# Token-major output projections with resident split weights in a two-layer hybrid decoder kernel

## The chip, the cores and the metric

The kernel is one program for one core of a Trainium2 chip. A core has a matrix engine (TensorE, PE in the rows, with PEld for its weight loads), VectorE (DVE), ScalarE (ACT), GpSimd (POOL) and SyncE (SP), which here mostly issues DMAs. The engines run their own instruction streams and meet at semaphores. The metric is device time in microseconds (us) of one execution. TensorE's clock has two levels, 1.2 and 2.4 GHz, and the profile gives the granted share of the upper one.

## The reference

A prompt of 1024 tokens and 8 samples of 8 tokens pass two layers, each `x + Mixer(RMSNorm(x))`, and a last RMSNorm. The kernel puts them side by side as T = 1088 tokens. What the change touches is the end of each mixer and what follows it:

```python
def rmsnorm(x, g):                       # x * rsqrt(mean(x^2) + 1e-6) * g
def retention_layer(...):                # layer 0
    ...
    o, s_new = chunked_linear_recurrence(q, k, v, log_a, s0)      # 4 heads, 512 values each
    o = _rms(o).reshape(b, L, 2048) * head_norm                   # one norm per head
    return (o * silu(gate)) @ w_out, s_new                        # w_out (2048, 1024)
def ssd_layer_full(...):                 # layer 1
    ...
    y, s_new = chunked_linear_recurrence(cm, bm, v, log_a, s0)    # 8 groups, 256 values each
    g = (y + xs * d_skip) * silu(z)
    g = _rms(g.reshape(b, L, 8, 256)).reshape(b, L, 2048) * gate_norm
    return g @ w_out, s_new, new_conv
def trunk(...):
    h = h + retention_layer(rmsnorm(h, ret_norm), ...)
    h = h + ssd_layer_full(rmsnorm(h, ssm_norm), ...)
    return rmsnorm(h, final_norm), ...
```

## The kernel before

Everything is float32. Large products are split: each operand is a high part rounded to the type fp32r and a low part, the remainder, and three fp32r matmuls (high x high, high x low, low x high) are summed. The program (`program`) runs its phases one after the other. Each phase is a block with one instruction stream per engine, and its end is a barrier for all of them.

Activations lie channel-major: the 128 partitions are channels, tokens run along the row, and in DRAM a tensor is (channels, T).

- `phase_input` turns x with TensorE, and its result is also written to `xT_dram` as the residual.
- `phase_project` (lines 230 to 610) is used four times (tags p1 to p4). It takes one block of 128 output channels after the other. For a block it loads the weights for all K input blocks, splits them (ScalarE copies to `whi`, VectorE subtracts to `wlo`, lines 376 and 524, two slots), and TensorE multiplies for every input block, pass and each of four stretches of 272 tokens (line 471). The weights are the stationary operand, the tokens stream. For p2 and p4 (K = 16, 8 output blocks) VectorE then adds the residual block (line 590) and SP stores it to `h1_dram` or `h2_dram`, channel-major.
- `phase_retention` goes through 4 heads x 8 chunks of 128 tokens, plus one chunk of 64 sample tokens per head, so 36 units, each with `y` in PSUM. VectorE gates it (line 1064, `r_gn`), ScalarE squares it, GpSimd and a ones-matmul sum the squares, ScalarE makes the root (Ln and Exp, lines 922 and 925), VectorE multiplies by it (line 1070, `r_gf`), ScalarE copies to `ghi` (line 929), and GpSimd subtracts to `glo` (line 995). `ghi` and `glo`, the split input of the next projection, stay in SBUF for all T tokens. GpSimd had multiplied the gates by the head norm before (line 990).
- `phase_norm_steps` loads `h1`, norms it (`norm_parts`: squares on ScalarE, pair sums on VectorE, ones-matmuls, root, then per block norm, high copy, and subtraction, alternately on VectorE and GpSimd at line 170), and computes the SSD step sizes from 32 columns of the input projection (line 1271).
- `phase_ssd` goes through 8 groups of 4 heads, 8 chunks plus a sample chunk each: 72 units. Per chunk VectorE makes the masks (lines 1748, 1750), adds the state (1826), the sample state (1808), forms the outputs (1770 to 1780) and the decayed scores (1761), and norms the chunk before (line 1799, `s_gf`). GpSimd makes values (1672), decays the state (1698), gates (1685, `s_gn`), scales the sample state (1715) and subtracts to `g2lo` (1689). On SP a chunk is four loads for the chunk four ahead and the sample state for the chunk two ahead (line 1416, slots `s_in`); each waits first, the former for `gated`, the latter for the use of the slot (`held`, which waits and adds one to a counter).
- `phase_output` loads `h2` by tiles of 128 tokens, turns them with TensorE, makes squares and root on ScalarE, norms on VectorE (line 1939) and stores y.
- `clear_semaphores` clears all semaphores that are in use, one instruction each on SP, in a block of its own; it is called once, after p2.

## Time and profile before

| | us |
|---|---|
| median of 3 runs (lowest, highest) | 2537.31 (2534.93, 2539.39) |
| the profiled execution: its time | 2532.14 |
| its span, first to last instruction | 2530.4 |

| stage | from, us | length, us |
|---|---|---|
| input, norm, p1 | 0 | 636 |
| retention | 636 | 334 |
| p2 | 970 | 201 |
| norm and SSD steps | 1171 | 80 |
| p3 | 1251 | 595 |
| SSD | 1846 | 447 |
| p4 | 2293 | 201 |
| output | 2494 | 36 |

Over the span TensorE is busy 88% (2238.6 us), VectorE 41%, ScalarE 31%, GpSimd 20%, and 291.87 MB are moved at a mean of 115 GB/s. A share over the whole span mixes stages with different limits, so the stages have to be read one by one. In the rows by stretches the columns are: stretch, length, busy us with instructions in brackets for PE, PEld, DVE, ACT and POOL, then the granted clock, the DMA engines' busy share, and GB/s. In timelines a row may merge several instructions of a kind (xN), and brackets at the end name the idle time before and what ended it. Matmul records are pipelined and overlap; their pace is read from the distance of their starts.

### The profile page before, as it was taken

Reading aid. Unit: us, or ns where it says so; the run is one execution under the profiler, and the core shown is the slowest. Engines: PE = TensorE matmul, PEld = TensorE weight load, DVE = VectorE, ACT = ScalarE, POOL = GpSimd, SP = SyncE. Lnnn points to the kernel's source line nnn. Section 1 sums busy time; section 2 is a strip of 40 time slices with the busy share of each in tenths; the row PEclk is TensorE's granted clock in tenths of the full one; section 3 lists DMA queues with packets and bytes.
Section 4 is the critical chain, followed back from the end, with each engine's and each line's share of the span. In section 5 each row is a group of like instructions: output and inputs, shape, how many; then the busy total and the mean of one; then the engine's idle time right before and its main releaser. Section 6 shows DMA issues by size and latency. Waiting matters only on the chain. (4 is left out here: it accounts for less than half of the span.)

```text
span 2530.4 us, 46071 instructions
## 1 busy us (share of the span) xinstructions
PE 2238.6 (88%) x16118; PEld 2090.5 (83%) x16118; DVE 1028.8 (41%) x1513; ACT 781.1 (31%) x1503; POOL 504.5 (20%) x747
## 2 busy tenths in 40 slices
PE   5999999999699988996699999999927777788996
PEld 4999999999466767996599999999926666667995
DVE  4354101111244442111412255555528888883112
ACT  5111111222233332001311134433326656662002
POOL 1222000000344441000200000000016666661000
PEclk8999999999899998998799999999958888888997
DMA  5222322221767654222122222222136665664215
GB/s 194 77 79 92 112 85 86 92 96 61 199 200 213 204 173 145 80 70 100 40 86 85 93 87 85 94 94 85 70 85 157 158 159 143 148 150 130 79 60 168
DMA packets 427452, 291.87 MB, mean 115 GB/s; under 512 B 115856, under 2 KB 388880, under 8 KB 427312
## 3 DMA queue, kind: packets, MB, share of 16 engines
q1 hardware_dynamic: 379560, 262.44, 34.9%
q10 hardware_dynamic: 47808, 28.32, 3.6%
q8 instruction: 52, 0.85, 0.1%
q14 instruction: 32, 0.26, 0.0%
HBM read 190.50 MB, written 100.20 MB: 115 GB/s over the span
## 5 line engine op out<-in xcount | busy, mean ns | idle before, releaser
L471 PE MATMUL p1acc_ps<-xn1hi,p1whi 128*128 128x272 f32 x1536 | 256.3, 289 | 12.1 <-DVE xn1lo L170 7.8
L471 PE MATMUL p3acc_ps<-xn2hi,p3whi 128*128 128x272 f32 x1536 | 255.6, 288 | 4.1 <-DVE p3wlo L531 4.1
L471 PE MATMUL p1acc_ps<-xn1lo,p1whi 128*128 128x272 f32 x1536 | 255.6, 288 | 0.0
L471 PE MATMUL p3acc_ps<-xn2lo,p3whi 128*128 128x272 f32 x1536 | 255.5, 288 | 0.0
L471 PE MATMUL p1acc_ps<-xn1hi,p1wlo 128*128 128x272 f32 x1536 | 255.4, 288 | 0.0
L471 PE MATMUL p3acc_ps<-xn2hi,p3wlo 128*128 128x272 f32 x1536 | 255.1, 288 | 0.0
L471 PEld LDWEIGHTS p1acc_ps<-xn1hi,p1whi 128*128 128x128 f32 x1536 | 216.3, 189 | 14.0 <-issue 9.0
L471 PEld LDWEIGHTS p3acc_ps<-xn2hi,p3whi 128*128 128x128 f32 x1536 | 216.3, 189 | 4.8 <-DVE p3wlo L531 4.8
L524 DVE TENSOR_TENSOR p1wlo<-p1raw,p1whi 128x1024 fp32r<-128x1024 f32 x47 | 57.6, 1225 | 398.2 <-ACT p1whi L376 398.0
L471 PEld LDWEIGHTS p1acc_ps<-xn1lo,p1whi 128*128 128x128 f32 x1536 | 216.6, 189 | 0.0
L471 PEld LDWEIGHTS p1acc_ps<-xn1hi,p1wlo 128*128 128x128 f32 x1536 | 216.6, 189 | 0.0
L471 PEld LDWEIGHTS p3acc_ps<-xn2lo,p3whi 128*128 128x128 f32 x1536 | 216.3, 189 | 0.0
L471 PEld LDWEIGHTS p3acc_ps<-xn2hi,p3wlo 128*128 128x128 f32 x1536 | 216.1, 188 | 0.0
L376 ACT ACTIVATE p1whi<-p1raw 128x1024 fp32r<-128x1024 f32 x47 | 49.8, 1060 | 373.3 <-PE p1acc_ps L471 373.1
L557 DVE SCALAR_TENSOR_TENSOR p3acc<-p3mid,params,p3acc 128x1024 f32<-128x1024 f32 x96 | 123.4, 1285 | 73.8 <-ACT p3acc L410 64.9
L524 DVE TENSOR_TENSOR p3wlo<-p3raw,p3whi 128x1024 fp32r<-128x1024 f32 x47 | 57.6, 1226 | 212.2 <-ACT p3whi L376 212.2
L376 ACT ACTIVATE p3whi<-p3raw 128x1024 fp32r<-128x1024 f32 x47 | 49.9, 1061 | 226.1 <-PE p3acc_ps L471 223.9
L471 PE MATMUL p2acc_ps<-g1hi,p2whi 128*128 128x272 f32 x512 | 85.9, 290 | 7.7 <-DVE p2wlo L531 7.7
L1517 PEld LDWEIGHTS s_xyps<-s_dec,s_v 128*128 128x128 f32 x512 | 74.4, 216 | 21.7 <-DVE s_dec L1761 18.3
L471 PE MATMUL p4acc_ps<-g2hi,p4whi 128*128 128x272 f32 x512 | 86.0, 290 | 6.6 <-DVE p4wlo L531 6.6
L1484 PE MATMUL s_crps<-s_sin,s_cm 128*128 128x256 f32 x128 | 46.0, 443 | 45.8 <-DVE s_sout L1808 30.6
L471 PE MATMUL p2acc_ps<-g1lo,p2whi 128*128 128x272 f32 x512 | 85.7, 290 | 0.0
(290 smaller groups left out, 4161.7 us busy)
## 6 DMA issues: line engine op xcount, KB each, us to landing
ret_proj<-p1res SPq DMA_DIRECT2D x48, 544.0 KB, 5.0
ssd_proj<-p3res SPq DMA_DIRECT2D x48, 544.0 KB, 2.7
p1raw<-in_ret_w_in SPq DMA_DIRECT2D x47, 512.0 KB, 4.7
p3raw<-in_ssm_w_in SPq DMA_DIRECT2D x47, 512.0 KB, 3.8
r_vg<-ret_proj SPq DMA_DIRECT2D x64, 256.0 KB, 3.5
r_sin<-in_state_ret SPq DMA_DIRECT2D x32, 512.0 KB, 5.2
out_ret_sample<-r_sout ACTq DMA_DIRECT2D x32, 512.0 KB, 4.8
s_zx<-ssd_proj SPq DMA_DIRECT2D x128, 128.0 KB, 2.3
```

The source lines that it names most:

```text
L376: nc.scalar.activation(whi[:, s, :, :], raw[:, s, :, :], ACT.Copy).then_inc(hi_done, 1)
L471: mm = nc.tensor.matmul(acc_ps[:, s, b, 0:TB], wt[:, s, k, :], x[:, k, b * TB:(b + 1) * TB], start=(k == 0 and j == 0), stop=(k == K - 1 a ...
L524: nc.vector.tensor_tensor(wlo[:, s, :, :], raw[:, s, :, :], whi[:, s, :, :], ALU.subtract).then_inc(lo_done, 1)
L557: nc.vector.scalar_tensor_tensor(ap, xp[:, w:w + SEQ], wc, ap, ALU.mult, ALU.add)
L1484: nc.tensor.matmul(cr_ps[:, 0:W], cm[:, c * NS:c * NS + P], s_in[:, s, :, :].rearrange("p h n -> p (h n)"), start=(c == 0), stop=(c == NCH ...
L1517: last = nc.tensor.matmul(y_ps[:, s, h // 2, :], padded(v[:, s, :], h), dec[:, s, h, :], start=(h % 2 == 0), stop=(h % 2 == 1))
```

## The change

The two output projections p2 and p4 become one new phase, `phase_mix`, and are token-major: the split gated values are the stationary operand (128 tokens), the weights stream in two halves of 512 output channels, and the result has tokens on the partitions. All 16 weight blocks are loaded, multiplied by the head norm, split and kept in SBUF; tiles 0 and 1 are multiplied while they arrive. `phase_retention` and `phase_ssd` no longer norm and split. They write the gated values to DRAM (`g_dram`) and the sums of squares from one partition (`ss_dram`), both stored by SP; three slots of `gn` and `ssr` are guarded by the stores' semaphores. `phase_mix` reads both per token tile, makes the roots, scales, splits, multiplies, adds the residual (also token-major, x itself in the first layer), norms the tile and writes h and, in the first layer, the normed tile turned back to channel-major (`xn_dram`). `phase_steps` loads that instead of norming. `phase_output` is gone, `xT_dram` too. `clear_semaphores` is called three times: after the retention, after the first mix, after the SSD.

```diff
 def phase_retention(...)
+                def store_gated(h, c, r):
+                    held(sp, q["gated"], 9 * h + c + 1 + B, passed)
+                    rows = g_dram[bass.ds(h * RDV, RDV), c * P:c * P + r]
+                    sp.dma_start(rows.rearrange("(k p) t -> p k t", p=P), gn[:, slot(c), :, 0:r]).then_inc(q[f"g_out{slot(c)}"], 16)
+
+                def store_sums(h, c, r):
+                    held(sp, q["ss_ev"], 9 * h + c + 1 + B, passed)
+                    sp.dma_start(ss_dram[bass.ds(h, 1), c * P:c * P + r], ssr[:, slot(c), 0:r]).then_inc(q[f"ss_out{slot(c)}"], 16)
...
-                def root(n, r):
-                def high(n, h, t0, r):
+                def take_sums(h, c, r):
+
+                    act.wait_ge(q["ss_mm"], 9 * h + c + 1 + B)
+                    act.wait_ge(q[f"ss_out{slot(c)}"], taken(h, c))
+                    nc.scalar.activation(ssr[:, slot(c), 0:r], ss_ps[0:1, 0:r], ACT.Copy).then_inc(q["ss_ev"], 1)
...
-                def norm_gates(h, gates, r):
-                def low(n, h, t0, r):
-                def norm(n, of, r):
 phase_ssd, SP, per chunk
                         if c + SL < NCH or more:
                             load_chunk(g + (c + SL) // NCH, (c + SL) % NCH, 9 * g + c + 1)
+                        store_gated(g, c, P)
+                        if c:
+                            store_sums(g, c - 1, P)
+                        elif not first:
+                            store_sums(g - 1, NCH, NS)
                         if c + 2 < NCH or more:
                             load_state(g + (c + 2) // NCH, (c + 2) % NCH, 8 * g + c + 1)
 phase_steps (was phase_norm_steps)
-                norm.load(sp)
+                for k in range(KD):
+                    sp.dma_start(xn[:, k, :], xn_dram[k * P:(k + 1) * P, :]).then_inc(arrived[k], 16)
-                norm.squares(act)
+                for k in range(KD):
+                    dma_wait(act, arrived[k], 1)
+                    nc.scalar.activation(hi[:, k, :], xn[:, k, :], ACT.Copy).then_inc(x_hi, 1)
...
+def phase_mix(nc, sb, ps, sem, tag, A, w, head_norm, NG, width, g_dram, ss_dram, resid, gain, h_dram=None,
+              turned_dram=None, y=None):
+    NT, PARTS, KP, WS = NCH + 1, 4, KI // 4, 2
...
+                def load_raw(k):
+                    if k >= WS:
+                        sp.wait_ge(wlo_done, k - WS + 1)
+                    sp.dma_start(raw[:, k % WS, :], w[k * P:(k + 1) * P, :]).then_inc(raw_in[k % WS], 16)
+                def load_part(t, i):
+                    if t >= 2:
+                        sp.wait_ge(lo_done, part(t - 2, i))
...
+                load_sums(0)
+                load_part(0, 0)
+                load_raw(0)
+                sp.dma_start(hn[:, :], head_norm.rearrange("(k p) -> p k", p=P), allow_slow_non_contiguous=True).then_inc(hn_in, 16)
+                load_sums(1)
+                load_part(1, 0)
+                load_raw(1)
+                for i in range(1, PARTS):
+                    for t in range(2):
+                        load_part(t, i)
+                    for k in range(KP * (i - 1) + 2, KP * i + 2):
+                        load_raw(k)
...
+                for t in range(NT):
+                    if t + 2 < NT:
+                        load_sums(t + 2)
+                        for i in range(PARTS):
+                            load_part(t + 2, i)
+                    store(t)
+                    if t + 2 < NT:
+                        load_resid(t + 2)
...
+                def products(t, k):
+                    r = rows[t]
+                    for j, (x, wt) in enumerate(((ghi, whi), (ghi, wlo), (glo, whi))):
+                        for cols in halves:
+                            last = nc.tensor.matmul(acc[0:r, t % 2, cols], x[:, t % 2, k, 0:r], wt[:, k, cols],
+                                                    start=(k == 0 and j == 0), stop=(k == KI - 1 and j == 2))
...
+                for t in range(2, NT):
+                    pe.wait_ge(added, t - 1)
+                    for i in range(PARTS):
+                        pe.wait_ge(lo_done, part(t, i))
+                        for k in range(KP * i, KP * (i + 1)):
+                            last = products(t, k)
...
+                            if i == 2:
+                                turn(t - 1)
...
+                def weight_high(k):
+                    dma_wait(act, raw_in[k % WS], k // WS + 1)
+                    nc.scalar.activation(whi[:, k, :], raw[:, k % WS, :], ACT.Copy, scale=hn[:, k:k + 1]).then_inc(whi_done, 1)
+                act.wait_ge(ready, 2)
+                dma_wait(act, hn_in, 1)
+                group_roots(0)
+                group_roots(1)
+                for i in range(PARTS):
+                    for t in range(2):
+                        high(t, i)
+                    for k in range(KP * i, KP * (i + 1)):
+                        weight_high(k)
...
+                def weight_low(k):
+                    dve.wait_ge(whi_done, k + 1)
+                    nc.vector.scalar_tensor_tensor(wlo[:, k, :], raw[:, k % WS, :], hn[:, k:k + 1], whi[:, k, :],
+                                                   ALU.mult, ALU.subtract).then_inc(wlo_done, 1)
...
+                for t in range(NT):
+                    r = rows[t]
+                    dve.wait_ge(mm, t + 1)
+                    dma_wait(dve, res_in[t % 2], t // 2 + 1)
+                    nc.vector.tensor_tensor(h[0:r, t % 2, :], h[0:r, t % 2, :], acc[0:r, t % 2, :], ALU.add).then_inc(added, 1)
+                    if t + 2 < NT:
+                        for i in range(PARTS):
+                            scale_part(t + 2, i)
+                    dve.wait_ge(root, t + 1)
+                    nc.vector.scalar_tensor_tensor(xn[0:r, t % 2, :], h[0:r, t % 2, :], ms[0:r, t:t + 1], gB[0:r, :],
+                                                   ALU.mult, ALU.mult).then_inc(normed, 1)
+                    if t + 2 < NT:
+                        for i in range(PARTS):
+                            low(t + 2, i)
...
 program
+        phase_retention(nc, sb, ps, sem, A, O, ret_dram, g1_dram, ss1_dram)
+        clear_semaphores()
+        phase_mix(nc, sb, ps, sem, "p2", A, A["ret_w_out"][0, :, :], A["ret_head_norm"][0, :], RH, RDV, g1_dram, ss1_dram,
+                  tokens(A["x_prompt"], A["x_sample"]), A["ssm_norm"][0, :], h_dram=h1_dram, turned_dram=xn_dram)
         clear_semaphores()
```

## Rows read from the trace of the kernel before

**Rows 1.** Busy time by stage, columns as told above.
```profile
636.00:970.00 334.00, 291.43 (x1584) 211.40 (x1584) 138.70 (x181) 118.31 (x261) 143.11 (x190) 0.93 0.65 193
970.00:1171.00 201.00, 194.49 (x1536) 194.27 (x1536) 28.58 (x19) 15.93 (x11) 0.33 (x1) 0.98 0.26 84
...
1846.00:2293.00 447.00, 317.94 (x1832) 268.23 (x1832) 343.08 (x841) 256.73 (x753) 265.62 (x429) 0.84 0.59 142
2293.00:2494.00 201.00, 195.09 (x1536) 194.87 (x1536) 28.67 (x19) 15.94 (x11) 0.01 (x1) 0.98 0.26 84
```

**Rows 2.** The same view inside a group of SSD chunks and between two groups.
```profile
2102.06:2132.10 30.04, 24.88 (x164) 20.52 (x161) 29.62 (x73) 21.88 (x64) 22.70 (x36) 1.00 0.73 176
2132.10:2153.26 21.16, 14.73 (x68) 12.82 (x69) 13.71 (x34) 10.04 (x30) 10.11 (x18) 0.68 0.50 119
```

**Rows 3.** Timeline of TensorE in p2: start, us, engine, line, operation, out<-in, shapes, count.
```profile
999.81 0.66 PE L471 MATMUL p2acc_ps<-g1hi,p2whi 128*128 128x272 f32 x4
...
1002.31 0.66 PE L471 MATMUL p2acc_ps<-g1hi,p2wlo 128*128 128x272 f32 x4
```

**Rows 4.** Timeline of TensorE in the retention, matmuls of 512 columns.
```profile
942.07 1.88 PE L806 MATMUL r_cr<-r_sin,r_qm 128*128 128x512 f32 x4
...
944.02 0.40 PE L813 MATMUL r_sb<-r_vlo,r_ktm 128*128 128x512 f32 x1
...
944.72 0.49 PE L767 MATMUL r_vps<-r_ident,r_vg 128*128 128x128 f32 x3
```

**Rows 5.** DMA issues: tensors, queue, count, KB each, median us from issue to landing.
```profile
p3raw<-in_ssm_w_in SPq DMA_DIRECT2D x47, 512.0 KB, 3.8
...
r_sin<-in_state_ret SPq DMA_DIRECT2D x32, 512.0 KB, 5.2
...
s_sin<-in_state_ssm SPq DMA_DIRECT2D x64, 128.0 KB, 3.6
...
r_hn<-in_ret_head_norm SPq DMA_DIRECT2D x1, 8.0 KB, 4.9
```

**Rows 6.** Groups of instructions: count | busy us, mean ns | idle before them.
```profile
L376 ACT ACTIVATE p3whi<-p3raw 128x1024 fp32r<-128x1024 f32 x47 | 49.9, 1061 | 226.1 <-PE p3acc_ps L471 223.9 <-DMA p3raw<-in_ssm_w_in 2.2
...
L1939 DVE SCALAR_TENSOR_TENSOR o_yt<-o_pt,o_ri,o_g 128x1024 f32<-128x1024 f32 x8 | 10.3, 1284 | 17.5 <-ACT o_ri L1928 17.5
```

**Rows 7.** Timeline around p2, all engines.
```profile
970.63 2.02 SPq L332 DMA_DIRECT2D p2raw<-in_ret_w_out  x4
...
1170.83 0.34 SPq L329 DMA_DIRECT2D h1T<-p2res  x1
1181.65 0.34 SPq L173 DMA_DIRECT2D n2ones<-const_ones  x1
```

**Rows 8.** Timeline of the norm and SSD steps stage.
```profile
1200.16 0.42 ACT L1190 ACTIVATE d_whi<-d_raw 128x256 fp32r<-128x256 f32 x1 [1.64 <-DMA d_seqcol<-const_seqcol]
...
1230.11 0.66 PE L1271 MATMUL d_acc<-xn2hi,d_wlo 128*128 128x272 f32 x4
```

**Rows 9.** Timeline of VectorE in the SSD stage, one chunk.
```profile
2066.37 1.06 DVE L1799 SCALAR_TENSOR_TENSOR s_gf<-s_gn,s_hn,s_ri 128x128 f32<-128x128 f32 x2
2067.35 0.60 DVE L1748 SCALAR_TENSOR_TENSOR s_dec<-s_cr,ncum,s_least 128x128 f32<-128x128 f32 x2
...
2068.87 0.41 DVE L1770 TENSOR_TENSOR s_yc<-s_xyps,s_er 128x256 f32<-128x256 f32 x1
...
2071.35 1.06 DVE L1799 SCALAR_TENSOR_TENSOR s_gf<-s_gn,s_hn,s_ri 128x128 f32<-128x128 f32 x2
```

**Rows 10.** Timeline of GpSimd, SP and TensorE in the same chunk.
```profile
2065.93 0.72 POOL L1685 TENSOR_TENSOR s_gn<-s_yd,s_zx 128x256 f32<-128x256 f32 x1
...
2069.39 0.37 SPq L1416 DMA_DIRECT2D s_sin<-in_state_ssm  x1
...
2069.09 0.67 PE L1484 MATMUL s_crps<-s_sin,s_cm 128*128 128x256 f32 x2 [0.76 <-DVE s_sout L1808]
...
2071.49 1.16 PE L1517 MATMUL s_xyps<-s_dec,s_v 128*128 128x128 f32 x8
```

More of the change, by code:

```diff
@@ L754, in _ @@
                         load_state(0, 1, 0)
-                with sp.Fori(0, RH - 1) as h:
+                group(0, first=True)
+                with sp.Fori(1, RH - 1) as h:
                     group(h)
                 group(RH - 1, more=False)
+                store_sums(RH - 1, NCH, NS)
+                for i in range(3):
+                    n = 16 * RH * (1 if i == 2 else NCH // 2) + B
+                    sp.wait_ge(q[f"g_out{i}"], n)
+                    sp.wait_ge(q[f"ss_out{i}"], n)
             @block.tensor
@@ L979, in _ @@
                 group(RH - 1, more=False)
[L980 to L981 removed]
+                take_sums(RH - 1, NCH, NS)
                 act.wait_ge(q["stored"], 16 * RH * NCH + B)
@@ L1219, in _ @@
             def _(dve):
-                norm.pairs(dve)
+                for k in range(0, KD, 2):
+                    dve.wait_ge(x_hi, k + 1)
+                    nc.vector.tensor_tensor(lo[:, k, :], xn[:, k, :], hi[:, k, :], ALU.subtract).then_inc(lo_even, 1)
                 dve.wait_ge(hi_done, 1)
@@ L1261, in _ @@
             def _(pe):
-                norm.sums(pe, tail_ps)
                 dma_wait(pe, loaded, 9)
@@ L1267, in _ @@
                 for k in range(KD):
-                    norm.ready(pe, k)
+                    pe.wait_ge(lo_odd if k % 2 else lo_even, k // 2 + 1)
                     for j, (wt, x) in enumerate(passes):
@@ L1444, in _ @@
                         load_state(0, 1, 0)
-                with sp.Fori(0, SG - 1) as g:
+                group(0, first=True)
+                with sp.Fori(1, SG - 1) as g:
                     group(g)
                 group(SG - 1, more=False)
+                store_sums(SG - 1, NCH, NS)
+                for i in range(3):
+                    n = 16 * SG * (1 if i == 2 else NCH // 2) + B
+                    sp.wait_ge(q[f"g_out{i}"], n)
+                    sp.wait_ge(q[f"ss_out{i}"], n)
             @block.tensor
@@ L1911, in _ @@
                     last.then_inc(turned, 1)
+                for i in range(PARTS):
+                    for t in range(2):
+                        if i == PARTS - 1:
+                            pe.wait_ge(lo_done, part(t, i))
+                            for k in range(KI - KP, KI):
+                                pe.wait_ge(wlo_done, k + 1)
+                                last = products(t, k)
+                            last.then_inc(mm, 1)
+                    if i < PARTS - 1:
+                        for k in range(KP * i, KP * (i + 1)):
+                            pe.wait_ge(wlo_done, k + 1)
+                            for t in range(2):
+                                if k == KP * i:
+                                    pe.wait_ge(lo_done, part(t, i))
+                                products(t, k)
@@ new lines, in _ @@
+                if turned_dram is not None:
+                    dma_wait(pe, consts, 2)
+                for t in range(2, NT):
+                    pe.wait_ge(added, t - 1)
+                    for i in range(PARTS):
+                        pe.wait_ge(lo_done, part(t, i))
+                        for k in range(KP * i, KP * (i + 1)):
+                            last = products(t, k)
+                        if i == PARTS - 1:
+                            last.then_inc(mm, 1)
+                        if turned_dram is not None:
+                            if t == 2 and i == 1:
+                                turn(0)
+                            if i == 2:
+                                turn(t - 1)
@@ L1913, in _ @@
+                if turned_dram is not None:
+                    turn(NT - 1)
             @block.scalar
@@ L1933, in _ @@
+                nc.vector.memset(eps[:, :], EPS).then_inc(ready, 1)
+                nc.vector.memset(eps_g[:, :], 4 * EPS).then_inc(ready, 1)
+                for i in range(PARTS):
+                    for t in range(2):
+                        scale_part(t, i)
+                    for t in range(2):
+                        low(t, i)
+                    for k in range(KP * i, KP * (i + 1)):
+                        weight_low(k)
                 dma_wait(dve, consts, 2)
```

417 lines of the change are left out of this document (209 added, 208 removed).

## The prediction

> **What bounds the kernel now.** I read the busy time by stage first [rows 1]. One core runs the stages one after the other, so what a change in a stage is worth is read from the engine that ends last in that stage. In the retention stage TensorE is busy 291 of 334 us, in the two output projections 194 of 201 us each. In the SSD stage no engine looks full (VectorE 343 of 447 us), but inside a group of eight chunks it is: 29.6 us busy of 30.0 us, and only the 21.2 us between two groups are loose [rows 2]. So the projections and retention are held by TensorE, the SSD chunks by VectorE, and the granted clock is 1.00 where TensorE streams and 0.68 between groups [rows 2].
>
> **Part 1, the two projections: the stream.** Before, a projection issues 8 x 16 x 3 x 4 = 1536 matmuls of 272 columns. Five groups of four later the timeline stands 2.50 us further [rows 3], so one costs 0.125 us and the stream 192 us. After, 9 token tiles x 16 x 3 x 2 = 864 matmuls of 512 columns. That is more columns (442 thousand against 418 thousand), because the last tile has 64 tokens and still streams all 512 columns. The trace has 512-wide matmuls of this type, the retention's split products: three of them take 0.70 us, 0.233 each [rows 4]; scaling rows 3 by columns gives 0.235. I take 0.235 (0.23 to 0.24): 203 us, which is 22.6 us a tile and 11 us more than before per projection. The first projection also turns its normed tiles, 8 transposes or 0.9 us a tile.
> The Trainium skill, "TensorE: Matmul & The Clock Gate", section "Step-by-step: what each phase is for", says a stream advances by one column per cycle and puts the gap between two 512-wide matmuls near 216 ns. By that the stream would be 187 us and this change 33 us cheaper over both projections. Rows 3 and 4 disagree, since 272 columns take 125 ns where the rule gives 116.
>
> **Part 1, the filling.** Before, weights for one output block are split while the block before is multiplied. After, all 16 weight blocks of 128 rows must arrive and be split while only tiles 0 and 1 exist to multiply (12 matmuls, 2.8 us, per block). The buffer for raw weights has two slots and a load waits for the subtraction of the block two before. One turn of the ring is therefore landing of 512 KB 3.8 us [rows 5], the copy 1.06 us and the subtraction 1.28 us [rows 6], and some 0.35 us of semaphore hops: 6.5 us for two blocks. Seven turns after the first pair are 45.5 us, where TensorE alone would need 38. With the landing of the busier retention stage, 5.2 us [rows 5], it is 55 us; I take 3.8 because little else moves then. Scaling and splitting of gated values falls into times in which both slots are in flight, cost nothing; with faster loads they would add some 2.8 us for each of three parts (four passes of half the size of the subtraction).
> Ahead of it: sums of squares as a broadcast, a gated part, the first weights and the per-row norm factors (2048 pieces of four bytes, 4.9 us to land [rows 5]) queue on one DMA ring, then two activations per tile. Summed along that ring the second block is ready 16 us after the first issue (13 to 19), in the second projection 18.5, whose broadcasts are twice as large. After block 15 the second tile still owes four blocks: 1.4 + 5.6 us, and 1 for the clock that falls in the waits. Tile 2 then waits about 1 us, since its splitting can only start when tile 0 is added.
> From there the operands of tile t+2 are ready about 10 us after tile t ends (add, root and norm 4.5, eight half-size passes 5.5), and they are used after 22.6, so these 7 tiles stream without holes. Loads, residual, norm and store hide there; if that cover fails, each costs its own latency of 4 to 8 us per tile.
>
> **Part 1, sums.** First projection: before 970.6 to 1181.7 = 211.0 us [rows 7]. After: 16 + 45.5 + 8 + 1 + 7 x 23.5 + a tail of 10.3 (add 1.3, square and root 1.8, norm 1.28 [rows 6], transposes, copy, store 3 to 4) = 245.3. The clears: before, some 121 semaphores are cleared between p2's last store and the next stage, 10.8 us [rows 7] less some 3.5 for the landing, 0.06 us each. After, 95 ahead of the stage and 36 behind, 5.7 + 2.8 us. Together 253.8, so +43. Second projection with output: before from 2293 to the end 237.1 us [rows 1] (201 us projection, 36 us output phase, which disappears because norm and store follow each tile). After: clear of 103 semaphores 6.2, then 18.5 + 45.5 + 8 + 1 + 7 x 22.6 + 8.2 = 245.6, so +8.5.
>
> **Part 2, the step before the SSD projection.** The squares, pair sums, root and norms of 1088-wide rows go; a load, a copy and a subtraction stay. The first engine to be late next is not the norm but the small loads behind eight large ones on SP: the step's weights are usable 18.5 us after the stage starts, and the matmuls end at 1230.8, 49 us after it [rows 8]. After, they start at about 18.6 us and need 8 x 1.5 us, one of them at half clock: end at 32.5. That is -16.5 us (-12 to -20).
>
> **Part 3, retention.** TensorE's chunk is full, the norm was beside it. ScalarE's two roots become one copy of one partition, which brings the samples' gate forward by an estimated 0.5 us a head: -2 us. Each chunk adds a 256 KB store and a small one on SP. Behind them stand only loads four chunks ahead and a state load with 6 us to spare; at worst +5 by contention (DMA share 0.65 already [rows 1]).
>
> **Part 4, SSD.** VectorE loses the norm: from its start to the next mask 0.98 us of a chunk of 5.0 us, the distance of two norms [rows 9]. That alone would give 4.05 us a chunk. What is late next is the state load. It is issued by SP 3.46 us after the gate of its chunk starts, as the last of five loads, and lands 3.6 us later [rows 5, 10]; it is used 8.2 us after that gate (3.16 and one chunk of 5.0), so there are 1.1 us to spare. The change puts two stores ahead of it on SP, each a hold, address arithmetic and issue of about 0.6 to 0.7 us by the spacing of the loads there. So it is issued at 4.8 and used at 8.5 at the earliest. From that use TensorE needs 2.4 us to the outputs matmuls [rows 10], 1.0 for them, and VectorE 2.2 to the next gate: 5.5. The loop spans three chunks, (8.5 + 5.5)/3 = 4.67 us. Also the DMA share of 0.73 inside a group [rows 2] would be near 0.9 with the stores at that pace, which lengthens the landing. Three of six steps still have loads ahead, so a group's 30.0 us become about 28.3, and the path between groups loses one norm, about 0.8 us because SP is busy then: 2.5 us x 8 = 20, and 1 for the small load that goes at the start: -21 us (-50 if only VectorE holds it, 0 if landings rise to 5 us).
>
> **Sum.** 43 + 8.5 - 16.5 - 2 - 21 = +12 us. The profiled execution took 2532.1 us (span 2530.4), so 2544; the median of the runs shown is 2537.3, 5 us above it, so 2549.5. A measurement of this kernel can tell about 0.2%, 5 us, from no change.
>
> **Rivals.**
> *SSD is released fully.* If SP's issues are short or the landing shrinks, the chunk goes to 4.1 us: 8 x (6 x 0.9 + 0.8) = 50 us instead of 21, total -17, 2520. For it: VectorE is the only full engine there. Against: 1.1 us of slack for 1.3 us of new issues.
> *512 columns stream at one per cycle.* The retention's plain matmuls do: four records, two matmuls, of 512 columns take 1.88 us, the last counted with its own 0.59, so 0.43 a record of two passes and 0.215 a pass [rows 4]. If the split products reached that in the new layout, 864 x (0.235 - 0.215) x 2 = -35, total -23, 2514. Against it: the split products in the same rows. (This is the outcome that the Trainium skill's section named above would have.)
> *The new projection starves.* Landings as in retention (5.2 us) make eight turns of the ring 1.4 us longer, in both projections +22, total +34, 2571. It decides from a landing above 3.8 us. For it: all loads of the filling share one ring with 512-byte rows of gated values.
> *The stores undo what the norm gives.* With DMA near full in SSD and retention no chunk gets shorter: +21 and +7, total +40, 2577.
>
> **How the numbers follow.** Forecast 0.48, full release 0.17, cheap columns 0.08, starved filling 0.17, stores undo 0.10. Of the forecast's own share a quarter lies within 5 us of no change and a tenth below. So faster 0.30 (0.17 + 0.08 + 0.05), within 0.2% 0.13, slower 0.57. The likeliest case alone spans 2537 to 2562. The range 2512 to 2580 leaves out the ends of the extreme cases.
>
> **What would show it.** Right: TensorE's 512-wide matmuls 0.235 us apart; first matmul of the new stage 13 to 19 us after its first load, weight blocks in pairs every 6.5 us, then 22.6 us a tile; no output phase; the step's matmuls over by 33 us; SSD chunks of 4.7 us with TensorE waiting for the state load in the later ones. Wrong: chunks of 4.1 us, tiles of 20.7 us, holes between tiles, or a retention stage that changed by more than 5 us.

## The result, and the profile after

The changed kernel takes 2565.8 us (median of 4 runs, 2559.3 to 2570.6) beside 2536.9 for the kernel before: ratio 1.0112, 95% interval 1.0084 to 1.014. It is 29 us slower, where the forecast said 12: inside the stated range, 4 us above the span of the likeliest case alone (2537 to 2562). Its profiled execution has a span of 2560.5 us, 30.1 above that of before.

Busy time by stage of the changed kernel; columns as in [rows 1]. The stretches are retention, first output projection, steps, SSD projection, SSD, second output projection with norm and store; each starts at its first load.

```profile
635.68:970.10 334.42, 291.80 (x1584) 212.78 (x1584) 114.42 (x144) 83.75 (x188) 64.45 (x118) 0.92 0.76 219
970.10:1226.54 256.44, 214.45 (x936) 169.01 (x936) 85.58 (x108) 72.59 (x116) 0.00 (x0) 0.91 0.45 131
1226.54:1281.92 55.38, 26.98 (x174) 23.52 (x174) 18.42 (x23) 17.48 (x23) 14.11 (x7) 0.65 0.30 99
1281.92:1883.28 601.36, 582.03 (x4640) 581.39 (x4640) 262.07 (x291) 194.16 (x263) 19.62 (x103) 0.98 0.27 87
1883.28:2317.28 434.00, 306.16 (x1832) 265.28 (x1832) 303.04 (x696) 204.39 (x608) 212.71 (x353) 0.85 0.66 165
2317.28:2560.50 243.22, 203.38 (x864) 159.05 (x864) 84.43 (x108) 71.50 (x107) 0.00 (x0) 0.93 0.45 129
```

The same stretches from first load to first load in both profiled executions. The forecast's clears stand here in the stage that they close (5.7 us behind the retention, 6.2 behind SSD).

| stage | before | after | difference | forecast |
|---|---|---|---|---|
| input, first projection | 639.3 | 635.7 | -3.6 | 0 |
| retention | 331.3 | 334.4 | +3.1 | +3.7 |
| first output projection | 211.0 | 256.4 | +45.4 | +37.1 |
| norm and steps | 69.9 | 55.4 | -14.5 | -16.5 |
| SSD projection | 601.5 | 601.4 | -0.1 | 0 |
| SSD | 440.2 | 434.0 | -6.2 | -14.8 |
| second output projection, output | 237.1 | 243.2 | +6.1 | +2.3 |
| sum | 2530.4 | 2560.5 | +30.1 | +12 |

The first row is scatter: no edit touches that stage, and in the traces of kernels that share it it took 635.7 to 642.7 us. What the forecast missed are 8 us in the first output projection, 9 in SSD, 4 in the second, 2 in the steps.

**The new stream.** TensorE in the second output projection, two matmuls a row (start, us, engine, line, operation, out<-in, shapes, count), and, in a second block, VectorE's additions, which follow the end of a tile:

```profile
2411.86 0.62 PE L1946 MATMUL p4acc<-p4whi,p4glo 128*128 128x512 f32 x2
...
2424.10 0.62 PE L1946 MATMUL p4acc<-p4whi,p4glo 128*128 128x512 f32 x2
```
```profile
2443.80 1.22 DVE L2086 TENSOR_TENSOR p4h<-p4h,p4acc 128x1024 f32<-128x1024 f32 x1 [14.52 <-PE p4acc L1946]
2465.56 1.22 DVE L2086 TENSOR_TENSOR p4h<-p4h,p4acc 128x1024 f32<-128x1024 f32 x1 [14.53 <-PE p4acc L1946]
```

27 pairs in 12.24 us are 0.2267 us a matmul, and a tile takes 21.76 us (22.66 with the transposes in the first projection): between the 0.235 of the forecast and the 0.215 of its rival.

**The filling.** VectorE's last two weight blocks in the first projection:

```profile
1029.15 1.28 DVE L2069 SCALAR_TENSOR_TENSOR p2wlo<-p2raw,p2hn,p2whi 128x1024 fp32r<-128x1024 f32 x1 [2.97 <-ACT p2whi L2014]
1032.01 1.28 DVE L2069 SCALAR_TENSOR_TENSOR p2wlo<-p2raw,p2hn,p2whi 128x1024 fp32r<-128x1024 f32 x1 [1.58 <-ACT p2whi L2014]
```

The second block is ready at 986.9, 16.8 us after the first issue (forecast 16), the last at 1033.29: 46.4 us for seven turns of the ring (forecast 45.5), 6.6 a turn.

**A hole that was not forecast.** The same projection, all engines around tile 2:

```profile
1055.59 1.03 PE L1956 MATMUL p2pt<-p2ident,p2xn 128*128 128x128 f32 x8
...
1057.71 0.36 SPq L1906 DMA_DIRECT2D xn2T<-p2xT  x1
...
1059.05 0.83 SPq L1887 DMA_DIRECT2D p2ri<-ss  x1
...
1064.62 0.72 ACT L2000 ACTIVATE p2ri<-p2ri,p2eps_g 128x512 f32<-128x512 f32 x1 [6.94 <-DMA p2ri<-ss]
...
1068.67 1.28 DVE L2091 SCALAR_TENSOR_TENSOR p2xn<-p2h,p2ms,p2gB 128x1024 f32<-128x1024 f32 x1
...
1070.01 1.97 PE L1956 MATMUL p2pt<-p2ident,p2xn 128*128 128x128 f32 x8 [7.93 <-DVE p2xn L2091]
```

Read it from below: TensorE waits 7.93 us inside tile 2 for the norm of tile 1. That norm stands on ScalarE behind the factors of tile 3; their sums were issued at 1059.05, since SP first had to store tile 0, and that store needs transposes which TensorE has inside tile 2. From its first matmul to that of tile 3, tile 2 took 35.8 us.

**The SSD chunk.** A steady chunk of the changed kernel: GpSimd, then VectorE, then TensorE's wait for the sample state, then the busy time of five such chunks (columns as in [rows 1]):

```profile
2185.37 0.73 POOL L1684 TENSOR_TENSOR s_gn<-s_yd,s_zx 128x256 f32<-128x256 f32 x1 [0.81 <-DVE s_yd L1767]
2186.05 0.66 POOL L1709 TENSOR_TENSOR s_smid<-s_sin,etot_s 128x256 f32<-128x256 f32 x1
```
```profile
2185.67 1.19 DVE L1735 SCALAR_TENSOR_TENSOR s_dec<-s_cr,ncum,s_least 128x128 f32<-128x128 f32 x2
...
2190.38 1.19 DVE L1735 SCALAR_TENSOR_TENSOR s_dec<-s_cr,ncum,s_least 128x128 f32<-128x128 f32 x2
```
```profile
2188.63 0.67 PE L1496 MATMUL s_crps<-s_sin,s_cm 128*128 128x256 f32 x2 [0.93 <-DMA s_sin<-in_state_ssm]
```
```profile
2180.65:2203.87 23.22, 18.28 (x127) 16.32 (x126) 22.87 (x51) 14.51 (x43) 15.12 (x25) 1.00 0.86 223
```

The chunk takes 4.71 us; 4.67 was forecast. But VectorE is busy 22.87 of 23.22 us. The norm (1.06 for two pieces, [rows 9]) is gone, and the mask behind it, 0.60 for two pieces there, now takes 1.19 and lies beside GpSimd's gate and its scaling of the sample state. The sign that the prediction had named, TensorE waiting for the state load, is there too. So a number came out right whose mechanism, the state load, was in doubt.

**The steps.** The same lengthening stands in the steps stage. The subtraction that gives the low part of the step's weights, in the kernel before (GpSimd idle) and in the changed one (GpSimd subtracts 128x1088 blocks beside it until 1245.7):

```profile
1200.61 0.43 DVE L1224 TENSOR_TENSOR d_wlo<-d_raw,d_whi 128x256 fp32r<-128x256 f32 x1 [0.76 <-ACT d_whi L1190]
```
```profile
1243.30 2.69 DVE L1211 TENSOR_TENSOR d_wlo<-d_raw,d_whi 128x256 fp32r<-128x256 f32 x1
```

TensorE waits for it, so these 2.3 us are about the 2 us that the forecast missed there. No run takes them away.

### The profile page after: what moved, and what is told of

It reads as the page before. It is cut to its first block and busy times, and to the rows that moved or that the text cites. A ratio compares the mean times of both kernels' runs of the same rounds, so it can differ in the third digit from the quotient of the medians.

```text
span 2560.5 us, 43366 instructions
## 1 busy us (share of the span) xinstructions
PE 2228.2 (87%) x14742; PEld 2009.1 (78%) x14742; DVE 1049.8 (41%) x1486; ACT 781.0 (31%) x1440; POOL 373.7 (15%) x603
## 5 line engine op out<-in xcount | busy, mean ns | idle before, releaser
L471 PE MATMUL p1acc_ps<-xn1lo,p1whi 128*128 128x272 f32 x1536 | 256.4, 289 | 0.0
L1946 PE MATMUL p4acc<-p4whi,p4ghi 128*128 128x512 f32 (+1 forms) x288 | 92.0, 401 | 40.6 <-DVE p4wlo L2069 36.1
L1946 PE MATMUL p2acc<-p2whi,p2ghi 128*128 128x512 f32 (+1 forms) x288 | 93.5, 406 | 31.8 <-DVE p2wlo L2069 29.4
L1946 PEld LDWEIGHTS p4acc<-p4whi,p4ghi 128*128 128x128 f32 (+1 forms) x288 | 52.5, 186 | 57.5 <-DVE p4wlo L2069 38.7
L1946 PE MATMUL p2acc<-p2whi,p2glo 128*128 128x512 f32 (+1 forms) x288 | 91.1, 398 | 0.0
L1946 PE MATMUL p2acc<-p2wlo,p2ghi 128*128 128x512 f32 (+1 forms) x288 | 90.6, 396 | 0.0
```

The lines of the kernel that those rows point to most:

```text
L471: mm = nc.tensor.matmul(acc_ps[:, s, b, 0:TB], wt[:, s, k, :], x[:, k, b * TB:(b + 1) * TB], start=(k == 0 and j == 0), stop=(k == K - 1 a ...
L1946: last = nc.tensor.matmul(acc[0:r, t % 2, cols], x[:, t % 2, k, 0:r], wt[:, k, cols], start=(k == 0 and j == 0), stop=(k == KI - 1 and j = ...
```

## Experiments

Times are medians; ratios are against the kernel before, measured beside it on the same chip. The median of the kernel before lay between 2533.4 and 2536.9 us beside the different runs, so where it matters a difference between two changed kernels is given by their ratios too. Lengths of stages are read from one trace each, and they scatter: the SSD stage of four kernels with the changed kernel's SSD code took 430.4 to 434.0 us. In the diffs "..." stands for lines left out.

### The state load first

```diff
+    if c + 2 < NCH or more:
+        load_state(g + (c + 2) // NCH, (c + 2) % NCH, 8 * g + c + 1)
     if c + SL < NCH or more:
         load_chunk(...)
     store_gated(g, c, P)
     ...
-    if c + 2 < NCH or more:
-        load_state(...)
```

> The changed kernel with one edit in the SSD stage: SP issues the state load of a chunk first, ahead of the four loads of a later chunk and of the two stores. Theory A (the state load holds the chunk, as the prediction had it): it is issued 4.65 us after the gate of its chunk starts in the changed kernel; ahead of the rest it can go some 3 us earlier, so the loop over three chunks (14.1 us) is no limit any more and the chunk falls from 4.71 us to what VectorE alone needs, about 4.1: 8 groups x 6 x 0.6 = 29 us less, about 2537. Theory B (VectorE holds the chunk, because the mask's two operations with both inputs in SBUF now run beside GpSimd's gate and take 1.19 us instead of 0.60): VectorE is busy 22.9 of 23.2 us already, the chunk stays at 4.7 us and the time within 5 us of 2566. Theory C (both limits stand at the same 4.7 us): the same as B here.

2571.2 us, ratio 1.0141 (1.0124 to 1.0158), SSD stage 434.5 us (434.0 in the changed kernel). SP, VectorE and TensorE in one chunk:

```profile
2238.29 1.19 DVE L1735 SCALAR_TENSOR_TENSOR s_dec<-s_cr,ncum,s_least 128x128 f32<-128x128 f32 x2
...
2239.63 0.39 SPq L1408 DMA_DIRECT2D s_sin<-in_state_ssm  x1
...
2240.62 0.67 PE L1496 MATMUL s_crps<-s_sin,s_cm 128*128 128x256 f32 x2 [0.37 <-DVE s_sout L1787]
```

The load goes out 1.64 us after its chunk's gate instead of some 4.6, TensorE no longer waits for it (0.9 to 1.0 us a chunk in the changed kernel), and the chunk stays at 4.71. Theory A, the forecast's, falls.

### The mask later

```diff
-    if following:
-        chunk_mask(g1, c1)
     dve.wait_ge(q["st_mm"], ...)
     ...
     # in outputs(), behind the product yc
+    chunk_mask(g1, c1)
```

> The changed kernel with one edit in the SSD stage: VectorE computes the next chunk's mask behind the states' sums and the first product of the outputs, at a time when GpSimd's gate and state decay are over; SP's order as in the changed kernel. Theory B (VectorE holds the chunk through operations lengthened by GpSimd): the mask's two pieces fall from 1.19 to 0.60 us, the chunk to 4.1 us, time about 2537. Theory A (state load) and theory C (both limits at 4.7 us): the mask's pieces fall to 0.60 us, but the chunk stays at 4.7 us and VectorE has 0.6 us idle in it; time within 5 us of 2566.

2606.3 us, ratio 1.0274 (1.0257 to 1.0291).

> Both edits in the SSD stage together: state load first on SP, mask later on VectorE. Theory C: only here does the chunk fall, to 4.1 us; 8 groups x 6 x 0.6 = 29 us, time about 2537. Theory A: no better than the state load first alone. Theory B: no better than the mask later alone. If all three kernels stay at 4.7 us, it is neither, and the DMA share of 0.86 inside a group would be next.

2606.4 us, ratio 1.0278 (1.026 to 1.0295), SSD stage 472.2 us. All three theories were wrong: the chunk grew to 5.42 us in both kernels. VectorE and GpSimd in the second of them:

```profile
2226.00 0.42 DVE L1790 TENSOR_TENSOR s_sout<-s_smid,s_sbps 128x256 f32<-128x256 f32 x1 [0.79 <-POOL s_smid L1709]
...
2226.59 0.61 POOL L1670 TENSOR_TENSOR s_v<-s_tok,dt_tok 128x256 f32<-128x256 f32 x1 [0.80 <-ACT s_tok L1578]
2226.67 1.30 DVE L1735 SCALAR_TENSOR_TENSOR s_dec<-s_cr,ncum,s_least 128x128 f32<-128x128 f32 x2
...
2227.16 0.66 POOL L1670 TENSOR_TENSOR s_vt<-s_tok,dtail 128x256 f32<-128x256 f32 x1
...
2227.89 0.83 DVE L1737 TENSOR_TENSOR s_dec<-s_cr,s_least 128x256 f32<-128x256 f32 x1
```

The mask was moved into GpSimd's next three operations: its two pieces take 1.30 us instead of the 0.60 hoped for (1.19 in the changed kernel), and its third, 0.41 there, takes 0.83. Besides, VectorE stood idle for 0.79 us where the mask had been. Against that, the two pieces of the outputs behind it, now clear of GpSimd, fell from 1.18 to 0.60. The edit tested a place, and the place was as bad; that it is the neighbour that counts had to be tested with the mask where it was.

### The mask's limit in PSUM

```diff
+ lim_ps = sc_ps[:, P:2 * P]          # free columns beside the scores
- mask(..., least[:, :], P)
+ mask(..., lim_ps, P)
  # TensorE, ahead of the scores
+ held(pe, q["dif"], n + 1 + B, passed)
```

> The changed kernel with one edit in the SSD stage: the mask's limit (a 128x128 constant) lies in PSUM beside the scores instead of in SBUF, so the mask's operations on VectorE have one input in SBUF, not two; TensorE's scores wait for the mask, which is done by then. The mask stays at its place beside GpSimd's gate. Theory D (an operation of VectorE with both inputs in SBUF is lengthened by a GpSimd operation that reads SBUF at the same time): the mask's two pieces fall from 1.19 to 0.60 us though GpSimd works beside them. The chunk falls by that to 4.1 us if the state load is no limit, or only to 4.67 us or a little below if the loop of the prediction (state load at 8.5 us plus 5.5 us over three chunks) holds it then. So 4.1: 2537; 4.67: 2564. Rival (they are slow for another reason, such as their place after the scores): 1.19 us as before, chunk 4.71 us.

2554.6 us, ratio 1.008 (1.0063 to 1.0097), SSD stage 426.9 us. The interval overlaps that of the changed kernel, so the evidence is in the trace:

```profile
2087.97 0.67 PE L1498 MATMUL s_crps<-s_sin,s_cm 128*128 128x256 f32 x2 [1.76 <-DMA s_sin<-in_state_ssm]
2088.16 0.73 POOL L1686 TENSOR_TENSOR s_gn<-s_yd,s_zx 128x256 f32<-128x256 f32 x1 [0.19 <-DVE s_yd L1769]
2088.47 0.60 DVE L1737 SCALAR_TENSOR_TENSOR s_dec<-s_cr,ncum,s_scps 128x128 f32<-128x128 f32 x2
```

Same place, same neighbours, one input in PSUM: 0.60. It holds for the whole stage: 126 of 128 such pieces take 0.34 us each, where in the changed kernel 115 of 128 take 0.54 us or more. Theory D stands. Early in a group a chunk takes 4.1 to 4.2 us; then the state load is late (TensorE waits for it 28 times, up to 2.5 us) and most chunks take 4.7 to 5.8. So the forecast's loop does exist by these waits: it comes in as soon as VectorE gives way.

### Both products and the state load

```diff
- tensor_tensor(yc[:, :, :], x_ps[...], er[...], ALU.mult)
+ tensor_tensor(x_ps[...],   x_ps[...], er[...], ALU.mult)
...
```

On top of the limit in PSUM, this kernel writes the product in place and issues the state load first.

> The same edit, and two more in the SSD stage: the product of the outputs is written back to PSUM in place of SBUF, so that the outputs' two pieces too have one input in SBUF; and SP issues the state load first. Theory D: these two pieces (1.18 us for both) fall to 0.60 too, so VectorE needs 4.71 - 0.59 - 0.58 = 3.5 us a chunk, TensorE 3.7 (18.3 us busy in 23.2), and the DMA engines, busy 0.86 of 4.71 us, 4.05 us: the chunk comes to 3.8 to 4.2 us, 8 x 6 x 0.6 = 29 us less or more, and the paths between groups a little: 2525 to 2540. Rival: the DMA engines or GpSimd hold the chunk above 4.4 us: 2550 or more.

2554.4 us, ratio 1.0083 (1.0058 to 1.0108), SSD stage 423.8 us (428.0 and 429.2 in two later kernels with the same SSD code): the rival, and no gain clear of the scatter over the kernel before it. What engines wait for in one group's later chunks (who, for what: us, times, longest):

```profile
PE s_tps L1469 <- DMA s_cr<-sums: 2.5, 3, 1.0
POOL s_gn L1686 <- DMA g2T<-s_gn: 2.5, 3, 1.1
```

A few chunks take 3.8 us, most 4.1 to 5.1. TensorE waits for no state load any more. The waits are now for the chunk's own loads and for the stores that this change added (a slot of gated values is not free yet).

### Without those stores

```diff
- sp.dma_start(rows..., gn[:, slot(c), :, 0:r]).then_inc(q[f"g_out{slot(c)}"], 16)
+ sp.sem_inc(q[f"g_out{slot(c)}"], 16)
...
```

> The kernel with the mask's limit and the outputs' product in PSUM and the state load first, and in the SSD stage the stores of the gated values left out (SP only counts them as done; the second projection reads the retention's gated values instead, so that its time stays). Theory F (the DMA engines hold the chunk, 0.91 busy with chunks of 4.4 us, and the change's own stores are what fills them): without the stores they need about what they needed before the change, 0.73 x 5.0 = 3.7 us, TensorE also 3.7; the chunk falls to 3.7 to 3.9 us and the SSD stage from 424 to 395 to 405 us. Rival (the chain through GpSimd and the semaphores holds it): the chunk stays at 4.3 us or more and the stage above 415 us.

2538.3 us (one run), SSD stage 410.1 us, 14 to 19 less than in the three kernels with the stores; the expectation said 19 to 29. Busy time of six chunks of it, and of the kernel with stores:

```profile
2161.56:2187.09 25.53, 22.39 (x162) 20.11 (x161) 21.86 (x61) 17.26 (x52) 17.62 (x30) 1.00 0.84 205
```
```profile
2172.33:2199.15 26.82, 22.90 (x162) 20.14 (x161) 22.40 (x61) 17.10 (x52) 17.71 (x30) 1.00 0.87 220
```

Half of the chunks take 3.7 to 3.8, every third 4.35 or more, with TensorE waiting for the chunk's load of broadcast sums (3.1 us in these six chunks); the mean is 4.25 against 4.47. Half of theory F holds. Why these loads are still late at a DMA share of 0.84 stays open.

### The norm alone, in the kernel before

```diff
- scalar_tensor_tensor(gf[:, k, 0:r], gn[:, slot, k, 0:r], hn[...], ri[:, 0:r], ...)
+ scalar_tensor_tensor(gf[:, k, 0:1], gn[:, slot, k, 0:1], hn[...], ri[:, 0:1], ...)
```

> The kernel before with one thing left out: in the SSD stage the norm on VectorE multiplies one column instead of all (the rest of the tile stays at one), so its two pieces take some 0.15 us in place of 1.05 and the gated values are not normed. Nothing is added: no store, no change on SP. It asks what the removal of the norm alone is worth. Theory of the prediction: VectorE's chunk falls by the norm's time to 4.1 us, and the state load, 1.1 us to spare before, gives (7.1 + 5.5)/3 = 4.2: chunk 4.2 us, 8 x 6 x 0.8 = 38 us less, 2499. Theory D (the mask slides beside GpSimd's gate and, with both inputs in SBUF, takes 1.19 us in place of 0.60): the chunk falls to 4.7 to 4.75 us only, 8 x 6 x 0.3 = 14 us less, about 2522.

2523.5 us (one run) beside 2534.5. GpSimd, then VectorE:

```profile
2118.22 0.73 POOL L1685 TENSOR_TENSOR s_gn<-s_yd,s_zx 128x256 f32<-128x256 f32 x1
2118.91 0.61 POOL L1715 TENSOR_TENSOR s_smid<-s_sin,etot_s 128x256 f32<-128x256 f32 x1
```
```profile
2118.66 0.88 DVE L1800 SCALAR_TENSOR_TENSOR s_gf<-s_gn,s_hn,s_ri 128x1 f32<-128x1 f32 x2
2119.46 0.60 DVE L1749 SCALAR_TENSOR_TENSOR s_dec<-s_cr,ncum,s_least 128x128 f32<-128x128 f32 x2
```

Two pieces, of one column each, take 0.88 us together; of 128 columns, they took 1.06. So of the 0.98 us that the forecast booked as the norm's, taking away the work gives back 0.18; the rest stays as a wait for GpSimd, left to whoever comes next. The chunk went from 5.0 to 4.81 us, not to the 4.2 of the prediction's theory, though nothing was added here that could delay the state load. (It is the one-column piece that waits and the mask stays at 0.60, not as theory D was put; its 4.7 to 4.75 and 2522 us were near.)

### Loads ahead of the store, in the projections

```diff
+ load_gated(2)
  for t in range(NT):
-     if t + 2 < NT:
-         load_sums(t + 2)
-         ...
+     load_gated(t + 3)
      store(t)
```

> The changed kernel with one edit in both output projections: SP issues the loads of sums of squares and gated values of tile t+3 ahead of the store of tile t, not behind it. In the first projection tile 2 takes 35.8 us where the others take 22.7, with 7.9 us of it a wait of TensorE for the norm of tile 1. Theory: that norm stands on ScalarE behind the norm factors of tile 3, whose sums SP issues only after the store of tile 0, which waits for the transposes that TensorE has inside tile 2; with the loads ahead of the store the wait goes, and with it what the fallen clock costs after it: 12 us less, 2554, tile 2 at 23 to 24 us. Rival (tile 1's norm is late for another reason: its residual, or ScalarE's work on tile 2): the wait stays above 5 us and the time within 5 us of 2566. The second projection has no transposes and no such wait, so it stays at 243 us in both.

2552.2 us, ratio 1.0069 (1.0053 to 1.0086): 14 us less (11 by the ratios). The first projection took 245.9 us instead of 256.4, the second 243.2 as in the changed kernel. VectorE's additions of tiles 1 and 2:

```profile
1048.57 1.22 DVE L2090 TENSOR_TENSOR p2h<-p2h,p2acc 128x1024 f32<-128x1024 f32 x1
1071.82 1.22 DVE L2090 TENSOR_TENSOR p2h<-p2h,p2acc 128x1024 f32<-128x1024 f32 x1 [4.26 <-PE p2acc L1950]
```

They lie 23.3 us apart, 34.3 in the changed kernel. The theory holds.

### The filling

```diff
- NT, PARTS, KP, WS = NCH + 1, 4, KI // 4, 2
+ NT, PARTS, KP, WS = NCH + 1, 4, KI // 4, 3
- sp.dma_start(hn[:, :], ...)     # SP
+ act.dma_start(hn[:, :], ...)    # ScalarE's queue
...
```

> The changed kernel with two edits in both output projections whose effects lie in different stretches. The ring of raw weights has three slots instead of two (the turned rows then one instead of two, to make room): if the ring is what holds the filling, as the prediction had it, the blocks 3 to 16 come at TensorE's pace of 2.72 us or at the loads' of some 2.0, no longer at 3.3, so the filling loses 5 to 8 us a projection. Rival (the splits of the gated values between the blocks or the shared DMA ring hold it): under 2 us. And the per-row norm factors, 2048 pieces of four bytes, are loaded by ScalarE's queue and not by SP's: SP's next issue took 4.1 and 5.9 us behind them, so the first block should come 3 to 5 us earlier in each projection; rival: the broadcast sums are the late ones and nothing moves. Sum for both theories: 2566 - 16 to 24 = 2542 to 2550.

2533.6 us, ratio 1.0006 (0.9995 to 1.0017): 32 us less than the changed kernel (27 by the ratios), more than the 16 to 24 expected, and no slower than the kernel before. What TensorE waited for in the first projection (us in total, times, longest; the longest is the wait for the first block and reaches back into the stage before): the changed kernel, then this one.

```profile
PE p2acc L1946 <- DVE p2wlo L2069: 29.4, 7, 23.8
```
```profile
PE p2acc L1945 <- DVE p2wlo L2069: 21.7, 1, 21.7
```

The projections took 241.5 and 227.2 us, 15 and 16 less. The first matmul came 2.0 and 3.6 us earlier; the other 12 to 13 us came with the third slot. After its first block TensorE never waits for one again. From the first matmul to tile 2, 57.2 us passed in the first projection of the changed kernel and 46.4 here, where 192 matmuls are 43.5. Of the 10.8 us saved there, 6.9 are TensorE's waits (8.0 against 1.1) and the rest is what stands behind them: behind the longest, 2.60 us, pairs took 1.05 us instead of 0.62 for 3.4 us, in which the granted clock was at its half level; behind the waits of 0.5 to 1.2 us they took 0.62 and the clock stayed full.

### Width

```diff
- halves = [slice(i * BANK, (i + 1) * BANK) for i in range(D // BANK)]
+ halves = [slice(i * 256, (i + 1) * 256) for i in range(D // 256)]
...
```

> The changed kernel with one edit in both output projections: each product streams 256 columns instead of 512, so twice as many matmuls for the same columns. It measures the term that the prediction mis-sized: 272 columns took 0.125 us and 512 columns 0.2267 us, where the prediction scaled by columns (0.235). Theory E (a matmul takes one column a cycle at 2.4 GHz and some 12 ns beside): 256 columns take 0.119 us, a tile of the second projection 22.8 us instead of 21.8, each projection some 9 us longer. Rival (time goes by columns alone, the new layout is cheaper for another reason): 0.1134 us and no change.

2571.7 us (one run). Four matmuls a row, and the additions of tiles 6, 7 and 8:

```profile
2450.57 0.64 PE L1946 MATMUL p4acc<-p4whi,p4glo 128*128 128x256 f32 x4
...
2461.13 0.64 PE L1946 MATMUL p4acc<-p4whi,p4ghi 128*128 128x256 f32 x4
```
```profile
2517.49 1.22 DVE L2086 TENSOR_TENSOR p4h<-p4h,p4acc 128x1024 f32<-128x1024 f32 x1 [15.80 <-PE p4acc L1946]
2540.53 1.22 DVE L2086 TENSOR_TENSOR p4h<-p4h,p4acc 128x1024 f32<-128x1024 f32 x1 [17.40 <-PE p4acc L1946]
2562.30 1.21 DVE L2086 TENSOR_TENSOR p4h<-p4h,p4acc 64x1024 f32<-64x1024 f32 x1 [17.48 <-PE p4acc L1946]
```

22 rows in 10.56 us: 0.120 us a matmul, a tile 23.04 us, as theory E said (0.119 and 22.8). But the last tile, of 64 tokens, takes 21.77: 0.1134, the rival's number. With 512 columns that tile gains nothing (0.230 us a matmul in the changed kernel). So in these traces a matmul of 256 columns costs more than half of one of 512 only with 128 tokens loaded, and theory E's constant is no constant. The projections grew by 4 and 3 us, not 9: the filling, bound by its ring, hid two tiles, and the last tile cost nothing more.

### Together

> All edits that gave something, together: in the projections the loads ahead of the store, three slots for raw weights and the norm factors from ScalarE's queue; in the SSD stage the mask's limit and the outputs' product in PSUM and the state load first. If the gains add up: 2566 - 14 (order) - 31 (filling) - 11 (SSD) = 2510, 1% faster than the kernel before. If the projections' two edits overlap (the wait in tile 2 takes in what the filling gave), 2520 to 2525.

2523.7 us, ratio 0.9936 (0.9915 to 0.9957): faster than the kernel before by 13 us, where the gains added up said 26. The first projection, 233.0 us, has nearly both its gains (23 of 25 us), the second, 227.5, the one that it can have. The SSD stage took 429.2 us with the same code that took 423.8 above, and the SSD projection 605.1 where most traces have 601; neither has a cause that I know. The next kernel has both again (428.0 and 604.9), and three of the SSD variants have the 605.

```diff
  @block.sync
-     for x in in_use: sp.sem_clear(x)
+     for x in in_use[0::4]: sp.sem_clear(x)
+ @block.scalar, @block.vector, @block.gpsimd: in_use[1::4], [2::4], [3::4]
```

> The kernel with all useful edits together, and the clears of the semaphores dealt out to four engines instead of SP alone. The prediction put 0.06 us on each: 95 ahead of the first projection, 36 behind it, 103 ahead of the second, 14 us in all. On four engines side by side 3.5 us are left: 10 us less, 2524 - 10 = 2514. Rival (the clears of one engine are not what takes the time between the stages, or other engines clear more slowly): within 3 us of 2524.

2513.4 us, ratio 0.9905 (0.9878 to 0.9932): 10 us less (8 by the ratios), as expected. The traces have it at its places: from the last store of the retention to the first load of the projection 5.1 us pass instead of 8.8, behind SSD 5.5 instead of 9.4. It is the fastest version, 21 us below the kernel before. The last edit would help the kernel before too; no run tests that.

## Why the prediction was right or wrong

The direction was right and the range held the time, but the difference was 2.4 times the forecast, and of the prediction's own signs of being wrong one came true, the hole between tiles. Its steps:

- **Clears, filling, tails: right.** In the first projection second block and ring came within 1 us, tail and clears within 2. In the other the second block came at 21.3 us instead of 18.5, the ring took 47.5 instead of 45.5, and tile 2 waited 4.4 us instead of 1, because the sums of tile 2 queue behind all loads of the filling: some 8 us in all. The rival of a starved filling had the right place and the wrong cause: landings were 3.6 and 3.8 us, as assumed; the third slot, not a faster landing, was what lacked.
- **The stream: mis-sized.** "Scaling rows 3 by columns gives 0.235" gave 203 us; at 0.2267 it is 196. Both [rows 3] and [rows 4] overstated it. For [rows 3], the experiment on width shows narrow matmuls with 128 tokens loaded paying an extra (0.120 instead of 0.1134 at 256 columns); why the retention's 512 columns took 0.233 stays open. That is 7 us a projection, 6 of them in its last seven tiles, two fifths of the way to the rival of cheap columns. The Trainium skill's page "TensorE: Matmul & The Clock Gate" ("Step-by-step: what each phase is for") has 216 ns for this gap; the trace has 226.7, so neither its number nor mine.
- **"These 7 tiles stream without holes": wrong.** The cover was looked for engine by engine, and no engine was late. What failed is an order: a store ahead of a load on SP, with the transposes it needs behind the wait that the load ends. It cost 13 us in tile 2 and hid the cheaper stream, so that the stage came out only 8 us off.
- **Retention: right sum, other terms.** Chunks stayed at 8.37 us. The first gate came 2.9 us sooner after the stage's start, which no step had; the likely cause, the norm factors' 2048 pieces [rows 5] that no longer queue there, was not tested. The three passages from head to head, forecast to shrink, grew by 2.5 us together: the samples' loads land some 0.8 us later and TensorE waits 2.9 to 4.6 us for them. That the sum agreed is luck.
- **Steps: right but for one overlap.** The weights were usable 15.7 us after the stage starts, yet the matmuls ran from 19.7 to 34.7, forecast 18.6 to 32.5, since the subtraction ahead of them took 2.69 us beside GpSimd and not the 0.43 of the kernel before.
- **SSD: the step that failed.** "VectorE loses the norm: from its start to the next mask 0.98 us of a chunk of 5.0 us", and "the state load is late next". Of these 0.98 us the mask, now beside GpSimd, took 0.59 over as a wait, so VectorE stayed the bound at 4.71; the state load, forecast as the bound at 4.67, was only just behind (issuing it first changed nothing while VectorE held the chunk, and it held most chunks at 4.7 and more once the mask's wait was gone). The chunk agreed by chance. Full release was refused for the wrong reason, and stores that undo the gain came true only in part, behind VectorE and the state load: they cost 14 to 19 us once both are out of the way. The paths between groups gained nothing (21.25 us on average in both kernels, forecast -0.8 each), and in some groups one chunk took 5.3 to 6.7.

The Trainium skill has the rule that I should have weighed: "SBUF — State Buffer", section "Who interferes with whom", says that VectorE's second SBUF input comes through a read port shared with GpSimd, so that such an operation and a GpSimd operation which reads SBUF block one another, while one with a single SBUF input does not. Both halves agree with these runs: 1.19 us with two inputs in SBUF, 0.60 with one, at the same place. It was visible in [rows 9] and [rows 10]: the norm's two pieces took 1.06 us beside the gate, the mask's, of the same shape, 0.60 behind it.

## What to carry to other kernels

Before booking an operation's duration as a gain, look at what runs beside it and at the same shape elsewhere: if it is longer there than here, the difference is a wait, and the next in line inherits it. A chunk with three limits within some 0.6 us gives up only what the nearest one allows, so each release must be costed up to the next. A wait that the profile shows is no proof of what holds the loop: TensorE's wait for the state load could be removed without any gain. And check a new pipeline for orders, not only for full engines: one store ahead of the loads on one queue cost 10 us of a projection.

## What was unexpected of the hardware

- Two VectorE operations, on a single column each, took 0.88 us together beside GpSimd's reads; two pieces of 128 columns take 0.60 where GpSimd is idle or one input lies in PSUM. The longest such case was a subtraction of 256 columns: 0.43 us alone, 2.69 beside GpSimd's subtractions of 1088 columns. All of it shows as busy time of VectorE, not as idle time.
- Matmuls of this type: 512 columns 0.2267 us with 128 tokens and 0.230 with 64, 256 columns 0.120 with 128 tokens and 0.1134 with 64.
- A third slot in a ring whose turn (6.6 us for two blocks) was only 1.2 us longer than TensorE's 5.4 gave 11 us in a filling of 57, of which 7 are waits: short waits cost more than their length, and the longest, 2.60 us, left the granted clock at its half level behind it (pairs of matmuls of 1.05 us instead of 0.62).
